# Linear attention in four chunks with a recurrent state, against one causal 256x256 score matrix per head

## The chip, the cores and the metric

The kernel runs on one core of a Trainium2 chip. The metric is device time in microseconds (us). The engines are PE (TensorE, matrix products), ACT (ScalarE), DVE (VectorE), POOL (GpSimd) and SP (SyncE, which issues the loads).

## The reference

Two transformer blocks over 256 tokens of width 2048, all in f32. The change touches one part of the second block, the gated linear attention: 4 heads, key width 256, value width 512, chunks of 64 tokens. Cut to what matters:

```python
def _gla_chunked(q, k, v, g):          # q is already scaled by 1/16
    b = jnp.cumsum(g, axis=2)          # within a chunk of 64
    b_mid = b[:, :, CHUNK // 2:CHUNK // 2 + 1]
    b_last = b[:, :, CHUNK - 1:CHUNK]
    a = jnp.einsum("bnihd,bnjhd->bnhij", q * jnp.exp(b - b_mid), k * jnp.exp(b_mid - b))
    a = jnp.where(jnp.tril(jnp.ones((CHUNK, CHUNK), dtype=bool)), a, 0.0)
    o_intra = jnp.einsum("bnhij,bnjhe->bnihe", a, v)
    q_in = q * jnp.exp(b)
    k_st = k * jnp.exp(b_last - b)
    decay = jnp.exp(b_last[:, :, 0])
    def step(state, xs):
        qn, kn, vn, dn = xs
        o = jnp.einsum("bihd,bhde->bihe", qn, state)
        state = state * dn[..., None] + jnp.einsum("bjhd,bjhe->bhde", kn, vn)
        return state, o
```

The output is o_intra plus the scanned o, then an RMS norm over the 512 values of a head, a gain and a gate.

## The kernel before

**Units.** Almost all of the run is matrix products of streamed weights. A *unit* is one 512 KB weight block of 512 x 256. SP loads it into one of five RAW slots (`load`, L326 to L345, which waits until the slot's earlier content was used); ACT rounds it to its high part WH (`act_split`, L433); DVE computes the low part WL (`dve_split`, L442); PE runs 8 pairs of matmuls (L394, L396) with it. WH and WL hold a ring of four units, so ACT and DVE split unit w + 4 in step w, and ACT's split waits until PE has finished unit w. Each engine has its own program in order. In one step w it does its part of the products, then the work placed beside unit w (`pe_beside`, `act_beside`, `dve_beside`). Four units make a pair of output tiles, which ACT (L509) and DVE (L534) move out of PSUM.

**The linear attention** rides beside the stages "og" and "g_a": 2 turns of 16 units each, one head per turn (heads 0, 1 in og, 2, 3 in g_a). `pe_linear_step`, `act_linear_step` and `dve_linear_step` get the unit w of the turn:

- w = 0 to 2: DVE and ACT make QMID, KMID (decays relative to the middle of a chunk), QIN, KEND (relative to its start and end) and DEND (a chunk's whole decay). L1441 ends that and raises gla_ready.
- w = 5: PE transposes KEND (L1310) and the values (L1314), and makes four 64x64 score blocks (L1320). ACT copies to KTOK, VTOK (L1382, L1383); DVE copies the causal half of the scores into AT (L1444).
- w = 8, 10, 12, 14: chunk c = 0 to 3. PE makes the state's new sum (L1337, not for c = 3) and per tile of 128 values the outputs, from AT (L1342) and from STATE (L1345, not for c = 0). DVE updates STATE (L1455, L1457).
- w = 14 and 15: ACT squares the output (L1386); PE sums the squares of four tiles with ONES (L1352); ACT takes Ln and Exp (L1390, L1392); DVE writes the normed output (L1464) and raises gla_normed.

In front of og stands `dve_decays` with the decay sums; behind og and g_a ACT applies Silu or Sigmoid to the stage's result (`act_gate`, L1476).

**The modulation** is a matrix-vector product on DVE, spread over the whole run: 12 blocks of 16 steps. A step (L1602, 1.3 us) takes one 512 KB load of its own through the same RAW slots. MOD_STEPS (L26 to L30) says at which units; a tuple gives units of each turn. `place_modulation` also places each block's end: PE sums over partitions (`pe_modulation`, L1613), one unit later DVE adds the bias (L1629). The sums go to a corner of OU[:, 1], which the linear attention uses too: so pe_modulation waits for gla_normed, and in head 2 PE's unit 5 waits for the block that ended in og (L1306).

```python
            total = unit + 2
            for name, following in (("og", "g_a"), ("g_a", "g_b")):
                if by_name[name].unit0 <= unit < by_name[following].unit0:
                    total = by_name[following].unit0 + 2
```

Of the kernel before, what the change touches and what calls it, by code (L numbers as in the profile page):

```python
# [11 lines left out]
P = 128  # L12
T = 256
# [14 lines left out]
    ("og", (3, 6, 9, 11, 14)), ("g_a", (3, 4, 6, 7, 9, 11, 13, 14)), ("g_b", 16), ("branch_a", 8),  # L28
# [188 lines left out]
def place_modulation(plan, stages, by_name):  # L217


    units = []  # L220
    for name, steps in MOD_STEPS:
        stage = by_name[name]
        if isinstance(steps, tuple):
            units += [stage.unit0 + i * stage.units + w for i in range(stage.turns) for w in steps]
            continue
        length = stage.pairs * stage.per_pair // (2 if name in ("mix_out", "down1") else 1)
        units += [stage.unit0 + (2 * j + 1) * length // (2 * steps) for j in range(steps)]
    assert len(units) == MOD_BLOCKS * KT
    plan.mod_steps, plan.mod_sums, plan.mod_adds = {}, {}, {}
    for n, unit in enumerate(units):  # L230
        plan.mod_steps.setdefault(unit, []).append(n)
        if n % KT == KT - 1:
            total = unit + 2
            for name, following in (("og", "g_a"), ("g_a", "g_b")):
                if by_name[name].unit0 <= unit < by_name[following].unit0:
                    total = by_name[following].unit0 + 2
            stage = next(stage for stage in stages if total < end_unit(stage))
            heads = stage.beside in ("diff", "mem", "win")
            if heads:
                total += (3 - (total - stage.unit0)) % stage.units  # L240
# [127 lines left out]
def pe_stage(pe, k, stage):  # L368
# [3 lines left out]
    def turn(i, last):  # L372
        for b in range(stage.body):
# [3 lines left out]
            for q in range(stage.per_pair):  # L377
# [21 lines left out]
                if stage.unit0 + i * stage.units + w in k.plan.mod_sums:  # L399
                    pe_modulation(pe, k, k.plan.mod_sums[stage.unit0 + i * stage.units + w], stage)  # L400
# [885 lines left out]
def blocks_before(k, name):  # L1286

    return sum(unit < k.plan.s[name].unit0 for unit in k.plan.mod_sums)
# [12 lines left out]
def pe_linear_step(pe, k, h, w):  # L1301

    if w == 5:

        pe.wait_ge(k.gla_ready, h + 1)
        if h == 2:  # L1306
            pe.wait_ge(k.mod_done, blocks_before(k, "g_a") + 1)
        for d in range(2):
            for tb in range(2):
                pe.transpose(k.SC[:, 0, tb * T + d * P:tb * T + d * P + P],  # L1310
                             k.KEND[:, d, tb * P:tb * P + P], k.IDENT[:, :])
        for e in range(GLA_DV_T):
# [12 lines left out]
    elif w in (8, 10, 12, 14):  # L1325
        c = (w - 8) // 2
        if c == 0:
            pe.wait_ge(k.gla_copied, h + 1)
            pe.wait_ge(k.gla_masked, h + 1)
        half, block = slice(64 * (c % 2), 64 * (c % 2) + 64), c // 2  # L1330
        if c:
            pe.wait_ge(k.state_ready, 3 * h + c)

            pe.wait_ge(k.chunk_out, 3 * h + c)
        if c < 3:
            for d in range(2):
                mm = pe.matmul(k.SC[:, d, :], k.KTOK[half, block, d * P:d * P + P],  # L1337
                               k.VTOK[half, block, :], start=True, stop=True)
            mm.then_inc(k.state_sum, 1)
        for e in range(GLA_DV_T):  # L1340
            out = k.OU[:, e // 2, (e % 2) * T + c * CHUNK:(e % 2) * T + c * CHUNK + CHUNK]
            mm = pe.matmul(out, k.VTOK[half, block, e * P:e * P + P],  # L1342
                           k.AT[half, block, :], start=True, stop=c == 0)
            for d in range(2) if c else ():
                mm = pe.matmul(out, k.STATE[:, d, e * P:e * P + P],  # L1345
                               k.QIN[:, d, c * CHUNK:c * CHUNK + CHUNK], start=False,
                               stop=d == 1)
        mm.then_inc(k.gla_out if c == 3 else k.chunk_out, 1)
    elif w == 15:
        pe.wait_ge(k.gla_squared, h + 1)  # L1350
        for e in range(GLA_DV_T):
            mm = pe.matmul(k.SC[:, 0, 0:T], k.ONES[:, :], k.OSQ[:, e, :], start=e == 0,  # L1352
                           stop=e == GLA_DV_T - 1)
        mm.then_inc(k.gla_summed, 1)
# [13 lines left out]
def act_linear_step(act, k, h, w, chain):  # L1368
# [11 lines left out]
    elif w == 5:  # L1380
        act.wait_ge(k.gla_turned, h + 1)
        act.activation(k.KTOK[:, :, :], k.SC[:, 0, :].rearrange("p (b d) -> p b d", b=2), ACT.Copy)  # L1382
        act.activation(k.VTOK[:, :, :], k.OU[:, :, :], ACT.Copy).then_inc(k.gla_copied, 1)  # L1383
    elif w == 14:
# [3 lines left out]
    elif w == 15:  # L1388
        act.wait_ge(k.gla_summed, h + 1)
        chain.link(act.activation(k.BREL[:, 0, :], k.SC[:, 0, 0:T], ACT.Ln,  # L1390
                                  scale=1.0 / (GLA_DV_T * P), bias=k.EPS[:, 0:1]))
        act.activation(k.BREL[:, 0, :], k.BREL[:, 0, :], ACT.Exp,  # L1392
                       scale=-0.5).then_inc(k.gla_rstd, 1)


def dve_decays(dve, k, chain):

    dve.memset(k.AT[:, :, :], 0.0)
# [24 lines left out]
def dve_linear_step(dve, k, h, w, chain):  # L1423
# [13 lines left out]
    elif w == 2:  # L1437
# [3 lines left out]
        dve.tensor_tensor(k.KEND[:, :, :], k.KEND[:, :, :], keys, ALU.mult).then_inc(k.gla_ready, 1)  # L1441
    elif w == 5:
        dve.wait_ge(k.gla_turned, h + 1)
        dve.copy_predicated(k.AT[:, :, :], k.TRIL[:, :, :].bitcast(I32),  # L1444
                            k.SC[:, 1, 0:P].rearrange("p (b i) -> p b i",
                                                      b=2)).then_inc(k.gla_masked, 1)
    elif w in (8, 10, 12):
        c = (w - 8) // 2
        dve.wait_ge(k.state_sum, 3 * h + (c + 1))
        if c:  # L1450
            dve.wait_ge(k.chunk_out, 3 * h + c + 1)
        for d in range(2):
            state = k.STATE[:, d, :]
            if c == 0:
                last = dve.tensor_scalar(state, k.SC[:, d, :], 1.0, None, ALU.mult)  # L1455
            else:
                last = dve.scalar_tensor_tensor(  # L1457
                    out=state, in0=state, scalar=k.DEND[:, 4 * d + c, :], in1=k.SC[:, d, :],
                    op0=ALU.mult, op1=ALU.add)
        last.then_inc(k.state_ready, 1)  # L1460
    elif w == 15:
# [144 lines left out]
def pe_modulation(pe, k, block, stage):  # L1606
# [3 lines left out]
    if stage.name in ("g_a", "g_b"):  # L1610
        pe.wait_ge(k.gla_normed, 2 if stage.name == "g_a" else GLA_HEADS)
# [55 lines left out]
def pool_second_constants(pool, k, chain):  # L1667
# [8 lines left out]
    pool.memset(k.TRIL[:, :, :], 1.0)  # L1676
# [7 lines left out]
    for half in range(2):  # L1684
        select(k.TRIL[64 * half:64 * half + 64, :, :], [[0, 2], [1, CHUNK]], 0, -1, 0.0,
               ALU.is_ge)
# [217 lines left out]
def make_semaphores(nc, k, ctx):  # L1904
# [29 lines left out]
    k.chunk_out = semaphore("chunk_out")  # L1934
# [34 lines left out]
    k.state_ready = semaphore("state_ready")  # L1969
    k.state_sum = semaphore("state_sum")  # L1970
    k.gla_out = semaphore("gla_out")
    k.gla_squared = semaphore("gla_squared")
    k.gla_summed = semaphore("gla_summed")
# [33 lines left out]
def place_buffers(nc, k, ctx):  # L2007

    base = (nc.sbuf_base + 63) // 64 * 64
    size = T * 4  # L2010

    class Region:
# [5 lines left out]
        def put(self, name, shape, dtype=F32, tile=0):  # L2018
# [36 lines left out]
    k.KTOK = y.put("KTOK", [P, 2, T], tile=6)  # L2055
    k.STATE = y.put("STATE", [P, 2, 2 * T], tile=8)
# [33 lines left out]
    k.GKL = dist.put("GKL", [P, T])  # L2090
    k.AT = nc.alloc_sbuf_tensor_at("AT", [P, 2, CHUNK], F32, offset=dist.start + size)
    k.TRIL = nc.alloc_sbuf_tensor_at("TRIL", [P, 2, CHUNK], F32,
                                     offset=dist.start + size + 2 * CHUNK * 4)
# [85 lines left out]
```

## Time and profile before

| | us |
|---|---|
| median of 3 runs | 2822.84 (2819.81 to 2824.84) |
| the profiled execution | 2834.41 |
| its span | 2832.7 |
| mean granted TensorE clock | 0.973 |
| busy in the span: PE, DVE, ACT, POOL | 2720.1 (96%), 1979.5 (70%), 1317.3 (47%), 11.5 (0%) |
| read from HBM | 551.18 MB, 195 GB/s over the span |

Busy time of PE counts overlapping matmuls once. The times of the profile belong to the one profiled execution, whose span is 0.4% above the median. "x4" behind a line is a count of instructions. PEclk is the TensorE clock that was granted, 1.00 for full speed.

### The profile page before, as it was taken

The page shows a single profiled execution, that of the slowest core. Times are in us where ns is not written, and L with a number is a line of the kernel's source. Part 1 is how long each engine was busy: PE and PEld are TensorE (multiplying, and loading weights), DVE is VectorE, ACT ScalarE, POOL GpSimd, SP SyncE. Part 2 cuts the span into 40 slices and gives each one's busy share as a digit, 9 for nine tenths or more (in the row PEclk, how much of TensorE's full clock was granted, in tenths as well). Part 3 has the DMA queues.
Part 4 walks back from the last instruction along what each step waited for, and adds up shares of the span by engine and source line. Part 5 has one row for each costly group of instructions (what it writes and reads, how often), then busy time and mean ns, then how long its engine had stood idle before and what let it go on. Part 6 is the DMA issues. An engine that isn't in the chain of part 4 may idle for free.

```text
span 2832.7 us, 38110 instructions
## 1 busy us (share of the span) xinstructions
PE 2720.1 (96%) x15225; PEld 2326.9 (82%) x15225; DVE 1979.5 (70%) x2606; ACT 1317.3 (47%) x1748; POOL 11.5 (0%) x63
## 2 busy tenths in 40 slices
PE   6999999999999998999999999999799999999997
PEld 6888888788888787888778888888688888888886
DVE  4777676777766777666555557878578887688864
ACT  5544555454555544454433444544444444444442
POOL 0000000000000100000000000000000000000000
PEclk9999999999999999999989999999899999999998
DMA  5687554678655476655345558888456669966662
GB/s 194 193 260 245 164 157 142 223 247 271 201 163 150 139 242 208 209 155 149 113 149 156 179 183 258 271 263 275 125 155 188 186 186 293 286 192 187 194 214 84
DMA packets 570762, 555.78 MB, mean 196 GB/s; under 512 B 18231, under 2 KB 545226, under 8 KB 569818
## 3 DMA queue, kind: packets, MB, share of 16 engines
q1 hardware_dynamic: 570586, 553.34, 63.3%
q8 instruction: 121, 1.98, 0.3%
q14 instruction: 55, 0.45, 0.0%
HBM read 551.18 MB, written 2.10 MB: 195 GB/s over the span
## 4 chain that ended last, share of the span: by engine, by line
PE 84%; DVE 9%; ACT 4%; issue 2%; SPq 0%; DMA 0%; POOL 0%; ACTq 0%; DVEq 0%; POOLq 0%
PE ACC L394 50%; PE ACC L396 25%; DVE WL L442 2%; ACT WH L433 1%; PE OU L1345 1%; PE OU L881 1%; ACT PROB L906 1%; PE SC L1337 1%; PE SC L649 1%; PE OU L1342 1%; PE SC L860 1%; PE SC L889 1%; PE OU L1613 1%; DVE PROB L936 1%; PE SC L848 1%
## 5 line engine op out<-in xcount | busy, mean ns | idle before, releaser
L394 PE MATMUL ACC<-XH,WH 128*128 128x512 f32 x6096 | 2198.9, 404 | 47.7 <-issue 22.1
L396 PE MATMUL ACC<-XH,WL 128*128 128x256 f32 x6096 | 1717.0, 282 | 0.0
L433 ACT ACTIVATE WH<-RAW 128x1024 fp32r<-128x1024 f32 x852 | 900.1, 1058 | 1318.1 <-PE ACC L396 1287.7
L442 DVE TENSOR_TENSOR WL<-RAW,WH 128x1024 fp32r<-128x1024 f32 x852 | 1035.7, 1221 | 682.8 <-ACT WH L433 680.0
L394 PEld LDWEIGHTS ACC<-XH,WH 128*128 128x128 f32 x6096 | 1159.7, 190 | 340.3 <-issue 44.0
L396 PEld LDWEIGHTS ACC<-XH,WL 128*128 128x128 f32 x6096 | 1165.0, 191 | 5.5 <-issue 3.8
L394 PE MATMUL ACC<-AH,WH 128*128 128x512 f32 x704 | 247.0, 396 | 0.0
L1602 DVE SCALAR_TENSOR_TENSOR MODACC<-RAWMOD,CACT,MODACC 128x1024 f32<-128x1024 f32 x180 | 230.3, 1279 | 0.0
L396 PE MATMUL ACC<-AH,WL 128*128 128x256 f32 x704 | 196.3, 279 | 0.0
L394 PEld LDWEIGHTS ACC<-AH,WH 128*128 128x128 f32 x704 | 132.1, 188 | 31.4
L396 PEld LDWEIGHTS ACC<-AH,WL 128*128 128x128 f32 x704 | 132.5, 188 | 0.1
L509 ACT ACTIVATE HIGH<-ACC 128x512 f32<-128x512 f32 (+1 forms) x211 | 113.1, 536 | 10.5 <-PE ACC L396 10.5
L529 DVE TENSOR_TENSOR PR<-ACC,HIGH 128x512 f32<-128x512 f32 x64 | 43.8, 684 | 2.3 <-ACT HIGH L509 2.3
L570 DVE SCALAR_TENSOR_TENSOR CV<-U,PARAM,CV 128x256 f32<-128x256 f32 x88 | 42.7, 485 | 3.1
L568 DVE SCALAR_TENSOR_TENSOR CV<-U,PARAM,CV 128x256 f32<-128x256 f32 x88 | 42.6, 485 | 3.1
L906 ACT ACTIVATE PROB<-PROB,NM 128x256 f32<-128x256 f32 x80 | 39.8, 499 | 5.9 <-DVE NM L945 4.6
L531 DVE TENSOR_TENSOR PR<-PR,RSTD 128x512 f32<-128x512 f32 x56 | 38.8, 692 | 1.9
L566 DVE TENSOR_SCALAR CV<-U,PARAM 128x256 f32<-128x256 f32 x88 | 36.4, 414 | 3.2
L565 DVE TENSOR_TENSOR U<-ACC,HIGH 128x256 f32<-128x256 f32 x88 | 36.8, 418 | 0.6 <-ACT HIGH L509 0.6
L649 PE MATMUL SC<-PR,ONES 128*128 128x256 f32 x64 | 20.8, 492 | 17.0 <-ACT PR L680 17.0
L543 DVE TENSOR_TENSOR SUM<-ACC,HIGH 128x512 f32<-128x512 f32 x40 | 27.4, 685 | 9.9 <-ACT HIGH L509 9.8
L1345 PE MATMUL OU<-QIN,STATE 128*128 128x64 f32 x192 | 33.6, 300 | 0.0
(254 smaller groups left out, 1362.8 us busy)
## 6 DMA issues: line engine op xcount, KB each, us to landing
RAW<-in_w_in SPq DMA_DIRECT2D x408, 512.0 KB, 4.5
RAWMOD<-in_w_mod SPq DMA_DIRECT2D x192, 512.0 KB, 4.8
RAW<-in_w_up SPq DMA_DIRECT2D x176, 512.0 KB, 4.6
RAW<-in_w_out SPq DMA_DIRECT2D x96, 512.0 KB, 4.8
RAW<-in_w_down SPq DMA_DIRECT2D x88, 512.0 KB, 4.8
RAW<-in_w_mem_kv SPq DMA_DIRECT2D x32, 512.0 KB, 4.3
RAW<-in_w_branch_gla SPq DMA_DIRECT2D x32, 512.0 KB, 5.0
RAW<-in_w_branch_attn SPq DMA_DIRECT2D x16, 512.0 KB, 5.0
```

The source lines that it names most:

```text
L394: pe.matmul(bank, k.WH[:, w % RING, kc, cols], x, start=tile == 0, stop=False)
L396: mm = pe.matmul(bank[:, 0:T], k.WL[:, w % RING, kc, cols], x[:, 0:T], start=False, stop=tile == tiles - 1)
L433: act.activation(k.WH[:, slot, :, 0:width], k.RAW[:, r % RAWS, :, 0:width], ACT.Copy).then_inc(k.hi_ready, 1)
L442: dve.tensor_tensor(k.WL[:, slot, :, 0:width], k.RAW[:, k.plan.unit_load[unit] % RAWS, :, 0:width], k.WH[:, slot, :, 0:width].bitcast(F32) ...
L509: act.activation(k.HIGH[:, first:stage.tiles], k.ACC[:, bank + first:bank + stage.tiles, T:2 * T], ACT.Copy).then_inc(k.high_ready, 1)
L529: chain.link(dve.tensor_tensor(dst, low, high, ALU.add))
L568: chain.link(dve.scalar_tensor_tensor(out=cv, in0=u[:, 1:1 + T], scalar=column(taps[1]), in1=cv, op0=ALU.mult, op1=ALU.add))
L570: dve.scalar_tensor_tensor(out=cv, in0=u[:, 0:T], scalar=column(taps[0]), in1=cv, op0=ALU.mult, op1=ALU.add).then_inc(done, 1)
L649: mm = pe.matmul(sums_of(k, n), k.ONES[:, :], squares_of(k, n, c)[:, f, :], start=c + f == 0, stop=c + f == 6)
L906: last = act.activation(k.PROB[:, g, :], source, ACT.Exp, bias=k.NM[:, g:g + 1], scale=scale, accum_out=k.SM[:, g:g + 1])
L1345: mm = pe.matmul(out, k.STATE[:, d, e * P:e * P + P], k.QIN[:, d, c * CHUNK:c * CHUNK + CHUNK], start=False, stop=d == 1)
L1602: dve.scalar_tensor_tensor(out=k.MODACC[:, :], in0=raw, scalar=c, in1=k.MODACC[:, :], op0=ALU.mult, op1=ALU.add).then_inc(k.mod_used, 1)
```

## The change

The state, its four sequential steps and the transposes of KEND go. In unit 5 PE now also computes the score blocks between different chunks: keys KEND of chunk c against QFAR, which holds the queries of all later chunks, decayed from the end of chunk c. DVE makes QFAR out of QIN and DEND ahead of gla_ready. All score blocks land in one bank of SC: 256 query columns for keys 0 to 127, and 128 query columns for keys 128 to 255. One masked copy takes them to AT, 384 columns wide, and in unit 8 PE applies them to all values: per value tile one matmul of 256 columns and one of 128. The square goes to unit 9 on ACT; DVE adds the four tiles of squares in unit 10; PE sums one tile in unit 11; Ln and Exp in unit 11, the normed output in unit 12. The last modulation steps of each turn move forward, and the blocks that end within og and g_a are summed in unit 14 of that turn.

```diff
-    ("og", (3, 6, 9, 11, 14)), ("g_a", (3, 4, 6, 7, 9, 11, 13, 14)), ("g_b", 16), ("branch_a", 8),
+    ("og", (3, 6, 7, 9, 12)), ("g_a", (3, 4, 6, 7, 8, 9, 11, 12)), ("g_b", 16), ("branch_a", 8),
...
             total = unit + 2
-            for name, following in (("og", "g_a"), ("g_a", "g_b")):
-                if by_name[name].unit0 <= unit < by_name[following].unit0:
-                    total = by_name[following].unit0 + 2
...
+            elif stage.beside == "gla":
+                total += (14 - (total - stage.unit0)) % stage.units
...
@@ pe_linear_step
         pe.wait_ge(k.gla_ready, h + 1)
-        if h == 2:
-            pe.wait_ge(k.mod_done, blocks_before(k, "g_a") + 1)
-        for d in range(2):
-            for tb in range(2):
-                pe.transpose(k.SC[:, 0, tb * T + d * P:tb * T + d * P + P],
-                             k.KEND[:, d, tb * P:tb * P + P], k.IDENT[:, :])
...
         for c in range(4):
-            half, block = slice(64 * (c % 2), 64 * (c % 2) + 64), c // 2
             for d in range(2):
-                mm = pe.matmul(k.SC[half, 1, block * CHUNK:block * CHUNK + CHUNK],
-                               k.KMID[:, d, c * CHUNK:c * CHUNK + CHUNK],
-                               k.QMID[:, d, c * CHUNK:c * CHUNK + CHUNK], start=d == 0,
+                pe.matmul(gla_scores(k, c, c, 1), k.KMID[:, d, c * CHUNK:c * CHUNK + CHUNK],
+                          k.QMID[:, d, c * CHUNK:c * CHUNK + CHUNK], start=d == 0, stop=d == 1)
+        for c, first in ((0, 0), (1, 3), (2, None)):
+            later = 3 - c
+            for d in range(2):
+                q = (k.QIN[:, d, 3 * CHUNK:] if first is None else
+                     k.QFAR[:, d, first * CHUNK:(first + later) * CHUNK])
+                mm = pe.matmul(gla_scores(k, c, c + 1, later),
+                               k.KEND[:, d, c * CHUNK:c * CHUNK + CHUNK], q, start=d == 0,
                                stop=d == 1)
         mm.then_inc(k.gla_turned, 1)
-    elif w in (8, 10, 12, 14):
...
+    elif w == 8:
+        pe.wait_ge(k.gla_copied, h + 1)
+        pe.wait_ge(k.gla_masked, h + 1)
         for e in range(GLA_DV_T):
+            out = k.OU[:, e // 2, (e % 2) * T:(e % 2) * T + T]
+            pe.matmul(out, k.VTOK[:, 0, e * P:e * P + P], k.AT[:, 0:T], start=True, stop=False)
+            mm = pe.matmul(out[:, P:T], k.VTOK[:, 1, e * P:e * P + P], k.AT[:, T:T + P],
+                           start=False, stop=True)
+        mm.then_inc(k.gla_out, 1)
+    elif w == 11:
+        pe.wait_ge(k.gla_presummed, h + 1)
+        pe.matmul(k.SC[:, 0, 0:T], k.ONES[:, :], k.OSQ[:, 0, :], start=True,
+                  stop=True).then_inc(k.gla_summed, 1)
+
+def gla_scores(k, keys, queries, count):
+    first = queries * CHUNK if keys < 2 else T + (queries - 2) * CHUNK
+    return k.SC[CHUNK * (keys % 2):CHUNK * (keys % 2) + CHUNK, 1, first:first + count * CHUNK]
...
@@ act_linear_step
     elif w == 5:
-        act.activation(k.KTOK[:, :, :], k.SC[:, 0, :].rearrange("p (b d) -> p b d", b=2), ACT.Copy)
...
-    elif w == 14:
+    elif w == 9:
         act.wait_ge(k.gla_out, h + 1)
...
-    elif w == 15:
+    elif w == 11:
         act.wait_ge(k.gla_summed, h + 1)
...
@@ dve_linear_step, w == 2
         dve.wait_ge(k.end_exps, h + 1)
-        dve.tensor_tensor(k.KEND[:, :, :], k.KEND[:, :, :], keys, ALU.mult).then_inc(k.gla_ready, 1)
+        chain.link(dve.tensor_tensor(k.KEND[:, :, :], k.KEND[:, :, :], keys, ALU.mult))
+        far = k.QFAR[:, :, :].rearrange("p d (c t) -> p d c t", c=5)
+        q = k.QIN[:, :, :].rearrange("p d (c t) -> p d c t", c=4)
+        ends = k.DEND[:, :, :].rearrange("p (d c) n -> p d c n", d=2)
+        dve.tensor_copy(far[:, :, 0:4:3, :], q[:, :, 1:3, :])
+        chain.link(dve.tensor_tensor(far[:, :, 1:5:3, :], q[:, :, 2:4, :],
+                                     ends[:, :, 1:3, :].broadcast_to([P, 2, 2, CHUNK]), ALU.mult))
+        dve.tensor_tensor(far[:, :, 2, :], far[:, :, 4, :],
+                          ends[:, :, 1, :].broadcast_to([P, 2, CHUNK]),
+                          ALU.mult).then_inc(k.gla_ready, 1)
     elif w == 5:
...
+        dve.copy_predicated(k.AT[:, :], k.TRIL[:, :].bitcast(I32),
+                            k.SC[:, 1, 0:T + P]).then_inc(k.gla_masked, 1)
+    elif w == 10:
+        dve.wait_ge(k.gla_squared, h + 1)
+        chain.link(dve.tensor_tensor(k.OSQ[:, 0:2, :], k.OSQ[:, 0:2, :], k.OSQ[:, 2:4, :], ALU.add))
+        dve.tensor_tensor(k.OSQ[:, 0, :], k.OSQ[:, 0, :], k.OSQ[:, 1, :],
+                          ALU.add).then_inc(k.gla_presummed, 1)
+    elif w == 12:
         dve.wait_ge(k.gla_rstd, h + 1)
...
@@ pe_modulation
-    if stage.name in ("g_a", "g_b"):
-        pe.wait_ge(k.gla_normed, 2 if stage.name == "g_a" else GLA_HEADS)
+    if stage.beside == "gla":
+        pe.wait_ge(k.gla_normed, head)
```

The rest of the diff follows from this: `pe_stage` passes the head to pe_modulation; the DVE steps that updated STATE (w = 8, 10, 12) and their semaphores are gone; TRIL, the mask, is [128, 384] now and POOL selects it in two pieces (columns 0 to 255 and the rest); in the SBUF, QFAR and AT take the place of KTOK and STATE, TRIL that of DIST, and GKL gets a region of its own.

## Rows read from the trace of the kernel before

**Rows 1.** The page's part 4, the chain that ended last, share by engine.
```profile
PE 84%; DVE 9%; ACT 4%; issue 2%; SPq 0%; DMA 0%; POOL 0%; ACTq 0%; DVEq 0%; POOLq 0%
```
**Rows 2.** Windows, four heads, then g_b: us, busy PE PEld DVE ACT POOL, PEclk, DMA, GB/s.
```profile
1424.25:1502.30 78.05, 77.65 (x403) 64.39 (x403) 43.40 (x51) 27.46 (x34) 0.00 (x0) 0.89 0.52 157
1502.30:1576.65 74.35, 73.44 (x401) 60.88 (x399) 35.58 (x42) 30.66 (x36) 0.00 (x0) 0.93 0.48 144
1576.65:1644.90 68.25, 68.25 (x386) 56.76 (x387) 40.38 (x47) 26.87 (x32) 0.00 (x0) 0.97 0.58 186
1644.90:1705.00 60.10, 60.10 (x340) 49.46 (x339) 35.20 (x38) 23.41 (x26) 0.00 (x0) 0.97 0.58 187
1705.00:1790.00 85.00, 85.00 (x487) 73.96 (x487) 62.66 (x59) 39.99 (x43) 0.00 (x0) 1.00 0.87 277
```
**Rows 3.** Windows of head 1: through chunk 0, and right behind chunk 1.
```profile
1511.95:1517.95 6.00, 6.00 (x31) 4.36 (x30) 3.62 (x5) 1.06 (x1) 0.00 (x0) 1.00 0.88 274
1526.95:1529.95 3.00, 3.00 (x11) 2.62 (x11) 1.41 (x2) 0.00 (x0) 0.00 (x0) 0.50 0.25 85
```
**Rows 4.** Chain in order of time, head 1: start us, us, engine, output, line, count.
```profile
1502.30 0.44 PE SC L1310 x4
1502.74 0.87 PE OU L1314 x8
1503.61 0.66 PE SC L1320 x16
...
1512.95 1.91 PE SC L1337 x4
1514.86 0.84 PE OU L1342 x8
...
1523.46 0.17 PE OU L1342 x2
1523.63 0.59 PE OU L1345 x4
1524.22 0.36 PE OU L1342 x2
...
1555.27 1.74 PE SC L1352 x8
```
**Rows 5.** Unit 13 of head 0 (ACT, DVE); group of L1345 weight loads, mean ns second.
```profile
1475.50 1.06 ACT L433 ACTIVATE WH<-RAW 128x1024 fp32r<-128x1024 f32 x1 [1.71 <-PE ACC L396]
1477.73 1.28 DVE L1602 SCALAR_TENSOR_TENSOR MODACC<-RAWMOD,CACT,MODACC 128x1024 f32<-128x1024 f32 x1
...
L1345 PEld LDWEIGHTS OU<-QIN,STATE 128*128 128x128 f32 x192 | 26.7, 201 | 3.3
```
**Rows 6.** PE in order of time, heads 0 and 2; in brackets idle us before it, releaser.
```profile
1427.62 0.66 PE L1310 MATMUL SC<-IDENT,KEND 128*128 128x128 f32 x4 [0.40 <-DVE KEND L1441]
...
1565.31 1.84 PE L1613 MATMUL OU<-ONES,MODACC 128*128 128x1 f32 x16
1576.65 0.63 PE L1310 MATMUL SC<-IDENT,KEND 128*128 128x128 f32 x4 [0.91 <-DVE MODS L1629]
```
**Rows 7.** DVE groups by form: count, busy us, mean ns of one, idle us before.
```profile
L664 DVE TENSOR_TENSOR PR<-PR 128x512 f32<-128x512 f32 x12 | 8.2, 685 | 0.0
L666 DVE TENSOR_TENSOR PR<-PR 128x256 f32<-128x256 f32 x12 | 5.1, 425 | 0.4
L1223 DVE COPY VS<-PR 128x256 f32<-128x256 f32 x12 | 3.5, 290 | 0.0
```
**Rows 8.** ACT and DVE in order of time: gates behind og, KEND of head 2.
```profile
1560.41 3.91 ACT L1476 ACTIVATE PR<-PR 128x1024 f32<-128x1024 f32 x4 [0.66 <-DVE PR L534]
...
1574.61 0.69 DVE L1441 TENSOR_TENSOR KEND<-KEND,PR 128x512 f32<-128x512 f32 x1
```
**Rows 9.** ACT groups: table loads in front of Ln; busy us, mean ns, idle us.
```profile
L1390 ACT ACT_TABLE_LOAD x2 | 2.6, 1283 | 0.0
```
**Rows 10.** DVE in order of time, in front of head 0.
```profile
1401.10 1.66 DVE L1401 TENSOR_SCALAR DECAY<-SC,PARAM 128x256 f32<-128x256 f32 x4 [7.21 <-PE OU L1296]
```

More of the change, by code:

```diff
@@ L399, in turn @@
                 if stage.unit0 + i * stage.units + w in k.plan.mod_sums:
-                    pe_modulation(pe, k, k.plan.mod_sums[stage.unit0 + i * stage.units + w], stage)
+                    pe_modulation(pe, k, k.plan.mod_sums[stage.unit0 + i * stage.units + w], stage,
+                                  stage.first + i + 1)
                 pe_beside(pe, k, stage, i, w)
@@ L1323, in pe_linear_step @@
+        for c, first in ((0, 0), (1, 3), (2, None)):
[5 more added lines that the diff above has]
+                               k.KEND[:, d, c * CHUNK:c * CHUNK + CHUNK], q, start=d == 0,
                                stop=d == 1)
         mm.then_inc(k.gla_turned, 1)
-    elif w in (8, 10, 12, 14):
[L1326 to L1339, printed above, removed]
-        for e in range(GLA_DV_T):
[L1341 to L1348, printed above, removed]
-    elif w == 15:
[L1350 to L1354, printed above, removed]
@@ L1387, in act_linear_step @@
                        ACT.Square).then_inc(k.gla_squared, 1)
-    elif w == 15:
+    elif w == 11:
         act.wait_ge(k.gla_summed, h + 1)
@@ L1396, in dve_decays @@
 def dve_decays(dve, k, chain):
-    dve.memset(k.AT[:, :, :], 0.0)
+    dve.memset(k.AT[:, :], 0.0)
     dve.wait_ge(k.decay_logits, 1)
@@ L1440, in dve_linear_step @@
         dve.wait_ge(k.end_exps, h + 1)
-        dve.tensor_tensor(k.KEND[:, :, :], k.KEND[:, :, :], keys, ALU.mult).then_inc(k.gla_ready, 1)
+        chain.link(dve.tensor_tensor(k.KEND[:, :, :], k.KEND[:, :, :], keys, ALU.mult))
[8 more added lines that the diff above has]
+                          ALU.mult).then_inc(k.gla_ready, 1)
     elif w == 5:
         dve.wait_ge(k.gla_turned, h + 1)
[L1444 to L1461, printed above, removed]
+        dve.copy_predicated(k.AT[:, :], k.TRIL[:, :].bitcast(I32),
[6 more added lines that the diff above has]
+    elif w == 12:
         dve.wait_ge(k.gla_rstd, h + 1)
@@ L1603, in dve_modulation, with pe_modulation @@
                                  op0=ALU.mult, op1=ALU.add).then_inc(k.mod_used, 1)
-def pe_modulation(pe, k, block, stage):
+def pe_modulation(pe, k, block, stage, head):
     pe.wait_ge(k.mod_used, KT * (block + 1))
     wait_from_zero(pe, k.mod_done, block)
-    if stage.name in ("g_a", "g_b"):
-        pe.wait_ge(k.gla_normed, 2 if stage.name == "g_a" else GLA_HEADS)
+    if stage.beside == "gla":
+        pe.wait_ge(k.gla_normed, head)
     for c in range(MOD_COLS // P):
@@ L1675, in pool_second_constants @@
     pool.memset(k.RESET[:, :], 1.0)
-    pool.memset(k.TRIL[:, :, :], 1.0)
+    pool.memset(k.TRIL[:, :], 1.0)
     for m in (k.DUP, k.DUPROT):
@@ L1683, in pool_second_constants @@
            ALU.not_equal)
-    for half in range(2):
-        select(k.TRIL[64 * half:64 * half + 64, :, :], [[0, 2], [1, CHUNK]], 0, -1, 0.0,
-               ALU.is_ge)
+    for first, count in ((0, T), (T, P)):
+        select(k.TRIL[:, first:first + count], [[1, count]], 0, -1, 0.0, ALU.is_ge)
     for parity in range(2):
@@ L1933, in make_semaphores @@
     k.gate_conv = semaphore("gate_conv")
-    k.chunk_out = semaphore("chunk_out")
     k.presummed = semaphore("presummed")
@@ L1968, in make_semaphores @@
     k.gla_masked = semaphore("gla_masked")
-    k.state_ready = semaphore("state_ready")
-    k.state_sum = semaphore("state_sum")
     k.gla_out = semaphore("gla_out")
     k.gla_squared = semaphore("gla_squared")
+    k.gla_presummed = semaphore("gla_presummed")
     k.gla_summed = semaphore("gla_summed")
@@ L2054, in place_buffers @@
     k.KEND = y.put("KEND", [P, 2, T], tile=4)
-    k.KTOK = y.put("KTOK", [P, 2, T], tile=6)
-    k.STATE = y.put("STATE", [P, 2, 2 * T], tile=8)
+    k.QFAR = y.put("QFAR", [P, 2, 5 * CHUNK], tile=6)
+    k.AT = y.put("AT", [P, T + P], tile=9)
     k.DECAYS = [None, y.put("DECAY1", [P, GLA_T // 2, T], tile=12)]
@@ L2089, in place_buffers @@
     k.DIST = dist.put("DIST", [P, 2, T])
[L2090 to L2093, printed above, removed]
+    k.TRIL = dist.put("TRIL", [P, T + P])
+    k.GKL = Region(size).put("GKL", [P, T])
     k.DISTI = pr.put("DISTI", [P, 2, T], I32, tile=44)
```

## The prediction, made before the changed kernel ran

> **What bounds the kernel now.** I read the page's chain first: what ended last is 84% TensorE (PE), so time that PE stops spending is time off the run unless something else comes late [rows 1]. The change touches only the two stages "og" and "g_a", which carry the four linear-attention heads, one head per sixteen units. Next the windows, one per head, from one head's transposes (unit 5) to the next's (the first from 1424.25, the last to just after g_a): 78.1, 74.4, 68.3 and 60.1 us, PE busy 98% or more of each, and a granted clock of only 0.89, 0.93, 0.97, 0.97 [rows 2]. A clock of 1.00 is the 2.4 GHz level and 0.50 the 1.2 GHz one. The reader should see two costs: work, and a clock lost. Time lost is length times (1 - clock): 8.6 + 5.2 + 2.0 + 1.8 = 17.6 us (each clock is rounded to 0.005, so within 0.4 us a head). A short window says where: right behind a chunk step of head 1 the clock is 0.50 with PE busy 3.00 of 3 us, while it is 1.00 through chunk 0 and what follows that [rows 3]. Then the chain of waits through head 1 gives the PE time of each piece of a head without the overlap that the busy figures hold [rows 4]. All f32 matmuls appear as two instructions; a transpose as one.
>
> **What is removed, per head, at full clock** [rows 4]. In unit 5: KEND transposes, 0.44. Chunk 0: state sums 1.91, outputs 0.84. Chunk 1 and chunk 2 each: state sums 1.91, then per value tile a pair on AT at 0.36 (the first, 0.17) and four on STATE at 0.59: 1.91 + 0.17 + 3 x 0.36 + 4 x 0.59 = 5.52. Chunk 3 has no state sum: 4 x 0.36 + 4 x 0.59 = 3.80. The square sums over four tiles: 1.74. Sum: 0.44 + 2.75 + 5.52 + 5.52 + 3.80 + 1.74 = 19.77 us. The eight V transposes (0.87) and the 16 near-score instructions (0.66) stay. That leaves, of head 2's 68.25 us, 68.25 - 19.77 - 1.53 - 2.0 (clock) = 44.95 for sixteen units of products, 2.81 each. As a check, head 1's window must then hold 44.95 + 21.30 + 5.2 (clock) + 0.91 (a wait) + 1.84 (a modulation sum) = 74.2; it is 74.35 [rows 2, 6].
>
> **What is added, per head.** Far scores in unit 5: six f32 matmuls, twelve instructions, with 192, 128 and 64 query columns, four of each. Unseen in this form. Square sums of 256 columns take 1.74/8 = 0.217 us each; near scores of 64 columns into halves of the partitions 0.66/16 = 0.041 [rows 4]. From below, 4 x (3 + 2 + 1) x 0.041 = 1.0; from above, all twelve at 0.217 = 2.6. I take width times 0.217/256: 4 x (0.163 + 0.109 + 0.054) = 1.3, since the many-column ones carry most. Outputs in unit 8: per value tile two instructions of 256 columns and two of 128. The first at 0.217. For 128 columns the neighbours are 0.109 by width (a transpose's 0.87/8 = 0.109 agrees) and 0.147, which 64-column matmuls with full weights take (0.59/4) [rows 4]; I take 0.147, as the weights must be loaded anyway: 4 x (0.434 + 0.294) = 2.9, between 2.6 and, all at 0.217, 3.5. Square sum in unit 11: two instructions, 0.43. Sum 4.63, between 4.0 and 6.5. **Work saved: 19.77 - 4.63 = 15.1 us a head, 60.5 us in four** (53 to 63).
>
> A rule to weigh: the 80 small instructions of the chunk outputs (8, then 3 x 24) cost 0.84 + 2 x 3.61 + 3.80 = 11.9 us a head by the chain, 0.148 each, while a weight load itself is shown with 201 ns [rows 4, 5]. The Trainium skill, "TensorE: Matmul & The Clock Gate", section "LDWEIGHTS (loading the stationary operand)", gives columns / 1.2 ns, 107 ns for 128 columns; priced so, an estimate, the 80 would be 8.6 us and the saving 3.3 us a head smaller, some 13 us in all (about 47 instead of 60.5). The trace disagrees with that price for f32 weights, and the measured rows stand.
>
> **Clock.** The 0.50 stretch of head 1 lies behind a chunk step of 24 small instructions after 1.9 us of state sums; chunk 0 (2.75 us) leaves the clock at 1.00 [rows 3, 4]. The change keeps one small-tile stretch of 0.87 + 0.66 + 1.3 = 2.8 us in unit 5 and puts 2.9 us of wide, full-array matmuls in unit 8. Both are about as long as chunk 0's, and half of the chunk steps' 5.5. I take 14 of the 17.6 us as returned; what stays is two losses of the size that heads 2 and 3 have now (1.8 us each) [rows 2]. Bounds: all 17.6, or nothing (as many drops behind the new steps).
>
> **DVE before unit 5.** Three operations join ahead of gla_ready, each behind a link or KEND: a 256-element copy (0.29), a 256-element product (0.42), a 128-element one (0.3, by width between nothing and the 256's) [rows 7], and two links: 1.1 us (0.7 to 1.5). Heads 1 and 3 hide it: DVE does this at unit 2 and PE asks after unit 5, and of the four heads only two show a wait there. Head 0 waits 0.40 us for KEND already, so +1.1. Head 2 is late as well, 0.91 us [rows 6]. There the chain runs: ACT and DVE finish head 1 (L1464), evacuate (L534), four Silu activations, then 11.0 us from their end (1564.32) to KEND's end (1575.3) [rows 8]. After the change L1464 is done in unit 12; after unit 15's products (1555.27 in the chain, the start of the square sums) come ACT's split, its copy and DVE's addition, and the Silus start some 3 us on instead of 5.1 [rows 4, 8]. Done: 3.0 + 3.9 + 11.0 + 1.1 = 19.0 after unit 15, while PE has six units, 16.9 us: wait 2.1 instead of 0.9, +1.2. The modulation sums (1.84) that PE did at head 2's unit 2 move to head 1's unit 14, at equal cost, and so does the block behind g_a.
>
> **The presum.** ACT squares in unit 9, DVE adds in unit 10, PE asks after unit 11. From the end of a unit's products, ACT's split ends at 1.15, DVE's at 2.3 (head 0's unit 13: ACT starts 1475.50, DVE's next work 1477.73) [rows 5]; two additions of 0.69 and 0.43 [rows 7] and a link make 3.5, while PE's unit is 2.81: 0.7 us of wait a head, 2.8 in all (0 to 6; DVE's modulation steps of units 8 and 9 could push it). Behind this wait on PE are units 12 on; their splits are four units ahead, so nothing else comes late.
>
> **Unit 14.** In head 3 Ln and Exp need two table loads of 1.28 [rows 9]; DVE's four gain products wait for them and the last modulation step of unit 12 is behind those. By the same stepping it ends 0.8 us after PE asks for it in unit 14: +0.8. In head 1 there are no loads, no wait.
>
> **At nothing:** removed state updates on DVE and the KTOK copy on ACT (under PE's units); the masked copy of 384 instead of 128 elements (three units to spare); DVE's larger memset (DVE waits 7.21 us behind it) [rows 10]; POOL's two wider selections (they lie with the other constants in the layer before). DMA: each moved modulation step takes its load along in SP's queue; in g_a ten unit loads and eight of these fall into units 3 to 12. The four-unit ring hides it: heads run at 144 to 187 GB/s and the next stage moves 277 with PE at 100% [rows 2]. Over g_a, 48 loads of 0.524 MB in two heads of 52 us are 242 GB/s. If that cover failed, DVE would wait in front of a modulation step, and its presum and evacuation behind it: rival (c).
>
> **Sum:** -60.5 - 14 + 1.1 + 1.2 + 2.8 + 0.8 = **-68.6 us**. The profiled execution took 2834.4 (span 2832.7), 0.4% over the median of 2822.84; on its own clock 2765.8, on the median 2754.2.
>
> **Rivals.** (a) *The clock does not come back*: the remaining steps drop it as often. Against: head 1's chunk 0 doesn't; for: unit 5's stretch gets 0.8 us longer and keeps its transposes. Then -54.6: 2768. Here belongs a rule: The Trainium skill, same page, section "Why this matters for your kernels", advises against idle gaps between bursts of matmuls to avoid throughput drops; by it alone these stretches, which have none, should lose no clock, and removing them should give none back. By that rule the result is this rival's 2768; the trace disagrees, since PE is busy 3.00 of 3.00 us at 0.50 [rows 3]. Chance 0.20. (b) *All clock back, no new wait* but head 0's: -77: 2746. For: DVE may run its link faster; against: stepping is plain. Chance 0.17. (c) *Loads or DVE become the bound in g_a*: modulation steps in units 6 to 9 hold DVE and its presum. DVE is busy 40 of 68 us in head 2 [rows 2] and would be about 39 of 52. At 4 us more per g_a head and 1 per og head, -59: 2764. Chance 0.10. (d) *Slower*: gla_ready comes so late that PE stands before unit 5 in each head. The break-even is 68.6/4 = 17 us a head against 1.1 us added to DVE's chain, so it needs an operation some ten times its row. 2830; chance 0.01. (e) *It doesn't do what it says*: PE's freed time is eaten by a hidden bound at half the gain: 2788; against, PE's 98% in every window. Chance 0.02. Forecast 0.50.
>
> **Range.** 2741 to 2776: from all clock back with the low added work, no new wait and the two old ones gone (-63 - 17.6 - 1.3 = -82) to no clock back and the added work at its upper bound (-53 + 5.9 = -47). It holds (a), (b) and (c); about 0.15 stays outside, (d), (e) and the tails. A measurement of this kernel tells about 0.2%, 5.6 us, from no change. Faster takes all cases but (d), 0.01, and 0.01 kept for a gain lost whole: 0.98, 0.01, 0.01.
>
> **What would show it.** Windows of og and g_a heads of about 52 us; the unit-8 group near 0.22 and 0.15 us an instruction; granted clock 0.98 or more; PE waits of 0.7 on DVE's addition in unit 11 and of about 1.5 and 2 before unit 5 in heads 0 and 2. A clock still near 0.93 makes (a) right; a PE wait on WL or a DMA wait in front of DVE's modulation (c). The forecast is wrong if the heads stay above 56 us, or if the stages behind g_a give time back.

## The result, and the profile of the changed kernel

The changed kernel takes 2759.99 us (median of 4 runs, 2757.4 to 2763.8) against 2821.57 for the one before: a ratio of 0.9765, 95% interval 0.9744 to 0.9787. That is 61.6 us less by the medians, 66 by the ratio; 68.6 was forecast (2754.2), with a range of 2741 to 2776. Sent again beside other runs, it gave 2757.81 against 2825.79, ratio 0.976 (0.974 to 0.9779).

The profiled execution took 2757.4 us, span 2755.5: 77 us under the profiled execution of before. The windows of the four heads, cut as in [rows 2] (us, busy PE PEld DVE ACT POOL, PEclk, DMA share, GB/s):

```profile
1421.20:1475.99 54.79, 52.84 (x325) 45.81 (x324) 39.94 (x50) 25.68 (x32) 0.00 (x0) 1.00 0.72 220
1475.99:1532.00 56.01, 53.12 (x327) 45.80 (x325) 34.24 (x43) 30.06 (x35) 0.00 (x0) 1.00 0.62 191
1532.00:1585.42 53.42, 52.72 (x312) 45.76 (x313) 40.11 (x46) 26.46 (x31) 0.00 (x0) 0.97 0.76 243
1585.42:1632.00 46.58, 45.29 (x287) 39.50 (x285) 34.65 (x38) 26.02 (x28) 0.00 (x0) 1.00 0.75 237
```

The heads are 51 to 56 us apart where they were 68 to 75, and the clock is 1.00 but for a dip in head 2. The windows average 52.7 us, where about 52 was forecast; head 1's, which holds a modulation sum and head 2's wait, is at the 56 that was named as the limit. PE now idles a little, though (head 1's window: 2.9 us). What it waited for, and the new work, in PE's order of time (heads 0, 2 and 3):

```profile
1424.59 1.09 PE L1308 MATMUL OU<-IDENT,PR 128*128 128x128 f32 x8 [1.19 <-DVE QFAR L1435]
1425.62 0.73 PE L1313 MATMUL SC<-QMID,KMID 128*64 128x64 f32 x16
1426.13 0.82 PE L1320 MATMUL SC<-QFAR,KEND 128*64 128x192 f32 x8
...
1447.55 0.70 PE L1335 MATMUL SC<-OSQ,ONES 128*128 128x256 f32 x2 [0.76 <-DVE OSQ L1445]
...
1531.99 1.09 PE L1308 MATMUL OU<-IDENT,PR 128*128 128x128 f32 x8 [2.08 <-DVE QFAR L1435]
...
1617.72 1.95 PE L1599 MATMUL OU<-ONES,MODACC 128*128 128x1 f32 x16 [0.54 <-DVE MODACC L1588]
```

The waits stand where the prediction put them: before unit 5 in heads 0 and 2 (1.19 and 2.08 us), in unit 11 (0.70 to 0.76 in each head), in unit 14 of head 3 (0.54). The chain gives the pieces without overlap, to be held against [rows 4] (start, us, engine, output, line, count):

```profile
1475.99 0.87 PE OU L1308 x8
1476.86 0.66 PE SC L1313 x16
1477.52 0.83 PE SC L1320 x11
...
1487.03 0.43 PE OU L1329 x2
1487.46 0.22 PE OU L1330 x2
```

The far scores take 0.83 us, the outputs, four times 0.43 + 0.22, 2.62 from the first to the next product, the square sum 0.43 (by the chain of the kernel narrow, below, where PE doesn't wait in front of it).

### The profile page after: what moved, and what is told of

Same layout as the page of the kernel before. It is cut to its first block, busy times and chain, and to the rows that moved or that the text cites. A ratio compares the mean times of both kernels' runs of the same rounds, so it can differ in the third digit from the quotient of the medians.

```text
span 2755.5 us, 37486 instructions
## 1 busy us (share of the span) xinstructions
PE 2635.5 (96%) x14929; PEld 2266.8 (82%) x14929; DVE 1972.4 (72%) x2602; ACT 1314.8 (48%) x1744; POOL 11.6 (0%) x63
## 4 chain that ended last, share of the span: by engine, by line
PE 82%; DVE 10%; ACT 5%; issue 2%; SPq 0%; DMA 0%; POOL 0%; ACTq 0%; DVEq 0%; POOLq 0%
PE ACC L393 50%; PE ACC L395 25%; DVE WL L442 2%; ACT WH L433 2%; PE OU L881 1%; ACT PROB L906 1%; PE SC L649 1%; DVE PROB L936 1%; PE OU L1599 1%; PE SC L860 1%; DVE MX L939 1%; PE SC L889 1%; DVE MODACC L1588 0%; PE SC L848 0%; DVE Y L1479 0%
## 5 line engine op out<-in xcount | busy, mean ns | idle before, releaser
L509 ACT ACTIVATE HIGH<-ACC 128x512 f32<-128x512 f32 (+1 forms) x211 | 113.1, 536 | 10.2 <-PE ACC L395 10.2
L529 DVE TENSOR_TENSOR PR<-ACC,HIGH 128x512 f32<-128x512 f32 x64 | 43.7, 683 | 2.3 <-ACT HIGH L509 2.3
L534 DVE TENSOR_TENSOR PR<-ACC,HIGH 128x512 f32<-128x512 f32 x46 | 31.4, 684 | 4.2 <-ACT HIGH L509 4.2
```

The source lines that it names most:

```text
L509: act.activation(k.HIGH[:, first:stage.tiles], k.ACC[:, bank + first:bank + stage.tiles, T:2 * T], ACT.Copy).then_inc(k.high_ready, 1)
L529: chain.link(dve.tensor_tensor(dst, low, high, ALU.add))
```

## The experiments

All ratios are to the kernel before, timed beside it on the same chip; the medians of different rows can come from different chips. "Clock lost in the heads" is length times (1 - granted clock), summed over windows of 2 us from the first head's scores to the end of the last head. It belongs to the one profiled execution.

| kernel | median us | ratio to before, 95% interval | clock lost in the heads, us |
|---|---|---|---|
| before, sent again | 2821.13 | 1.0006 (0.9989 to 1.0023) | 10.2 (first profile 17.1) |
| changed, sent again | 2757.81 | 0.9760 (0.9740 to 0.9779) | 3.4 (first profile 1.7) |
| split_steps | 2828.34 | 1.0025 (1.0004 to 1.0047) | 10.2 |
| wide | 2816.51 | 0.9988 (0.9968 to 1.0008) | 1.7 |
| narrow | 2821.17 | 0.9997 (0.9978 to 1.0016) | 12.0 |
| narrow13 | 2809.98 | 0.9927 (0.9902 to 0.9952) | 1.7 |
| chunk_shape | 2840.60 | 1.0056 (1.0034 to 1.0079) | 18.8 |
| old_mod | 2754.97 | 0.9734 (0.9710 to 0.9757) | 0.0 |
| presum9 | 2757.89 | 0.9758 (0.9739 to 0.9778) | 6.8 |
| scores6 | 2758.44 | 0.9763 (0.9739 to 0.9787) | 1.7 |
| both | 2753.45 | 0.9738 (0.9718 to 0.9759) | 1.7 |
| sum15 | 2747.27 | 0.9712 (0.9686 to 0.9738) | 0.0 |

**Both kernels again.** No edit.

> The kernel before once more, with its own profile. Theory 1 (its clock loss in the heads varies between executions, and the first profile, 0.4% above the median, caught a bad one): a loss well under 17.6 us, 5 to 13, with a span near 2820. Rival (the loss is fixed, and the profiled execution was long for another reason): 17 to 18 us again.

> The changed kernel once more, as the yardstick for the three runs beside it. Theory 1 (the profiles of before and after differ by their clock losses in the heads, which vary from one execution to the next): about 2760 us, 60 to 66 us under before, and in the profile a clock loss in the four heads of 0 to 4 us, not always behind the same unit. Theory 2 (a fixed loss tied to head 2's wait): 1.7 us lost in head 2 again and nothing elsewhere.

Before lost 10.2 us in the heads this time and 17.1 in the first profile, and its span was 2820.3. So the first profile had caught an execution with much clock lost: 7 us more in the heads, and 7 more in front of them, where both kernels are the same. The changed kernel lost 3.4 us, at other places than in its first profile: behind head 0's unit 5, where PE had waited 2.09 us, and behind head 3's modulation sum. Head 2's wait, 2.09 us as well, passed without a dip. So the dips are not tied to head 2, but they do go with the length of the wait: over all profiles of this study, PE waited 2.04 to 2.09 us in front of unit 5 nine times, and eight times the clock fell to the 1.2 GHz level there; of thirteen waits of 0.40 to 1.70 us in the same place none was followed by a fall. The 14 us more of lost clock in the first profile of before are why the two first profiles differ by 77 us and the medians by 62 to 68.

**split_steps.** The kernel before, cut differently. PE's state sums stay in units 8, 10 and 12; the outputs of the four chunks come in units 8, 11, 13 and 14, and DVE updates STATE in units 8, 11 and 13:

```diff
-    elif w in (8, 10, 12, 14):
+    elif w in (8, 10, 11, 12, 13, 14):
...
+        if w in (8, 11, 13, 14):
...
-    elif w in (8, 10, 12):
+    elif w in (8, 11, 13):
```

> The kernel before, with the outputs of chunks 1 and 2 moved one unit behind their state sums (units 11 and 13), so that no stretch of small matmuls is longer than 3.8 us; nothing is left out. Theory 1 (a long stretch of small matmuls lowers the clock): most of the loss in the heads goes, 6 to 14 us less than before, at the same PE work. Rival (what counts is the narrow work as such, however it is cut): as before within 3 us.

The rival was right about the clock: the loss is what the uncut kernel lost in its second profile, 10.2 us. The time is 0.25% longer, some 7 us and more than the rival's 3; the two more interruptions a head explain about 2 of them by the rows, the rest is open. A window over the outputs alone of head 0's chunk 1, 3.8 us of work from 1447.1, and what follows (same columns as above):

```profile
1448.00:1457.00 9.00, 9.00 (x37) 7.43 (x37) 4.43 (x5) 0.94 (x3) 0.00 (x0) 0.62 0.38 110
```

PE is busy throughout, and yet the clock averages 0.62: outputs without the state sums directly in front of them are enough to lower it. The first profile of before already showed this, and the prediction passed over it: chunk 3 has no state sums, and behind its 3.8 us of outputs in head 0 (from 1475.33) stands

```profile
1480.00:1482.00 2.00, 2.00 (x8) 1.71 (x8) 0.00 (x0) 0.47 (x1) 0.00 (x0) 0.50 1.01 314
```

In the profiles of before, before_again and split_steps together, the clock fell at or behind 8 of 20 such stretches of outputs alone.

**wide and narrow.** Work is added to the changed kernel in units 10, 12 and 14, its results unused:

```diff
@@ wide
+    elif w in (10, 12, 14):
+        for n in range(13):
+            pe.matmul(k.SC[:, 1, 0:T], k.VTOK[:, 0, (n % 4) * P:(n % 4) * P + P], k.AT[:, 0:T],
+                      start=True, stop=True)
@@ narrow
+    elif w in (10, 12, 14):
+        for d in range(2):
+            pe.matmul(k.SC[:, 1, :], k.VTOK[0:64, 0, d * P:d * P + P], k.VTOK[0:64, 0, :],
+                      start=True, stop=True)
+        for e in range(GLA_DV_T):
+            for n in range(3):
+                pe.matmul(k.SC[:, 1, n * CHUNK:n * CHUNK + CHUNK],
+                          k.VTOK[:, 0, e * P:e * P + P], k.AT[:, n * CHUNK:n * CHUNK + CHUNK],
+                          start=True, stop=True)
```

> As the narrow one, but each of the twelve additional pieces is thirteen f32 matmuls of 256 columns with full weights, about 5.6 us; its results are not used. Theory 1: 12 x 5.6 = 68 us more than the changed kernel and a clock of 1.00 behind them. Rival (any interruption of the products by 5 us lowers the clock): the same loss as the narrow one, 5 to 17 us on top.

> The changed kernel with additional work in units 10, 12 and 14 of each head, shaped like a chunk step of before: two f32 matmuls of 512 columns with 64 rows, then twelve of 64 columns with full weights; its results are not used. At full clock 12 x 5.5 = 66 us more than the changed kernel. Theory 1 (narrow matmuls lower the clock): 5 to 17 us on top of that, and a clock of 0.50 behind these steps in the profile. Rival (the clock comes back for another reason, such as the state's updates on DVE being gone): nothing on top.

The wide pieces lower nothing behind them: 5.6 us of interruption by full-width matmuls leaves the clock alone, and the loss of 1.7 us is again one dip at head 2's unit 5, where PE waits for QFAR. Their cost, 64 us by the ratios (59 by the medians, which come from different chips), is the 68 of work less the 3 us of unit-11 waits that the longer unit 10 covers. With the narrow pieces 12.0 us were lost, 1.7 of them again at head 2's unit 5, but not as theory 1 had it. A piece was cheaper than a chunk step, 24 instructions in 2.82 us instead of 3.61, and ten of the twelve left the clock at 1.00. It fell only at the two in unit 14 that came right behind a modulation sum (a wide piece in the same place left it at 1.00, both times). Chain and window of such a plain piece, then the window over a piece beside a sum:

```profile
1523.32 1.91 PE SC L1335 x4
1525.23 2.82 PE SC L1339 x24
```
```profile
1525.23:1531.00 5.77, 5.77 (x41) 5.36 (x42) 3.35 (x6) 0.00 (x0) 0.00 (x0) 1.00 0.57 155
1535.30:1546.00 10.70, 10.70 (x39) 8.46 (x39) 0.86 (x1) 0.00 (x0) 0.00 (x0) 0.56 0.28 89
```

**narrow13 and chunk_shape.** The first moves the third narrow piece to unit 13. The second keeps units 10, 12, 14 and gives the twelve narrow matmuls the rows of a real chunk step; its two matmuls of 512 columns use rows 64 to 127 instead of 0 to 63:

```diff
@@ narrow13
-    elif w in (10, 12, 14):
+    elif w in (10, 12, 13):
@@ chunk_shape, in place of the loop over n
+            out = k.SC[:, 1, 0:CHUNK]
+            pe.matmul(out, k.VTOK[half, 0, e * P:e * P + P], k.AT[half, CHUNK:2 * CHUNK],
+                      start=True, stop=False)
+            for d in range(2):
+                pe.matmul(out, k.VTOK[:, d, e * P:e * P + P],
+                          k.QIN[:, d, CHUNK:2 * CHUNK], start=False, stop=d == 1)
```

> The narrow one with its third piece in unit 13 instead of 14, so that none stands next to a modulation sum. Theory 1 (in the narrow one the clock fell only where a piece followed the sum's sixteen one-column matmuls): no loss behind the pieces, under 3.5 us in the heads against 12.0. Rival (it falls behind any piece now and then): two or three drops again at other places.

> As the narrow one, but with the row counts of a real chunk step: of the twelve 64-column matmuls behind the two of 512 columns, four use 64 rows and eight use 128, alternating as before. Theory A (mixing 64-row and 128-row matmuls is what slows the pieces and lowers the clock): 24 instructions take 3.6 us instead of the narrow one's 2.9, and the clock is at 0.50 behind three or more steps besides those next to a modulation sum; 8 us of work more than the narrow one and a loss of 8 to 17 us in the heads. Theory B (the 64 columns do it, whatever the rows): as the narrow one, drops only beside the modulation sums.

Both came out as theory 1 and theory A said. With no piece beside a modulation sum the loss is 1.7 us, all of it at head 2's unit 5. With the rows mixed it is 18.8 us, but not all of that is due to the mixing: 1.7 us are head 2's unit 5, and 10.2 stand at the two pieces beside a modulation sum, about what the narrow kernel lost there too. What the mixed rows add is the 6.8 us behind four of the ten pieces that stand alone; of the narrow kernels' 22 pieces that stand alone none was followed by a fall.

This does not hang on one profile: the whole run's granted clock was 0.980 or 0.981 in all four runs of narrow13, 0.975 to 0.978 in all ten of narrow and 0.971 to 0.975 in all eight of chunk_shape. By the ratios chunk_shape takes 17 us more than narrow, which has its pieces in the same units: 9.5 us of work (12 x 0.79) and 6.8 of clock.

The chain of chunk_shape in head 1, and the window right behind it:

```profile
1515.31 1.91 PE SC L1336 x4
1517.22 0.17 PE SC L1340 x2
1517.39 0.59 PE SC L1343 x4
1517.97 0.36 PE SC L1340 x2
1518.34 0.59 PE SC L1343 x4
```
```profile
1521.00:1524.50 3.50, 3.50 (x13) 3.02 (x12) 0.00 (x0) 0.00 (x0) 0.00 (x0) 0.52 0.11 39
```

It repeats the old pattern of [rows 4] number for number. A pair with 64 rows takes 0.36 us between pairs with 128 rows, and 0.17 directly behind another with 64; the narrow instructions that all use 128 rows take 2.82/24 = 0.117 each. In all, the 24 mixed instructions take 3.61 us and the 24 plain ones 2.82: some 0.2 us for each of the four times that PE goes into 64 rows and back, 0.8 us per chunk step. The Trainium skill, "TensorEngine Tiling (Array Packing)", section "Tiling Modes", says that changing the tiling mode drains TensorE; this trace agrees with that, by those 0.2 us, though it does not show a drain as such. More differs between the two kernels: the moving operand of eight matmuls (QIN instead of AT), their accumulation, and the rows of the 512-column matmuls. None was tried alone, so that it is the row count is likely and not shown. The greater length of a mixed piece (5.5 us against 4.7) is not needed to lower the clock, since the mixed outputs alone do it in 3.8 us.

**old_mod.** The changed kernel with MOD_STEPS, the place of the sums and their waits as before:

```diff
-    ("og", (3, 6, 7, 9, 12)), ("g_a", (3, 4, 6, 7, 8, 9, 11, 12)), ("g_b", 16), ("branch_a", 8),
+    ("og", (3, 6, 9, 11, 14)), ("g_a", (3, 4, 6, 7, 9, 11, 13, 14)), ("g_b", 16), ("branch_a", 8),
...
```

> The changed kernel with the modulation put back: steps at the old units, sums at unit 2 of the next stage, head 2 waiting for the block's end. Theory 1 (moving it cost nothing and gained nothing, as forecast): 2758 within 4 us; 1.84 us of PE work returns to head 2's start, where PE waited 2.1 us anyway. Rival (the move is a part of the gain): 3 to 8 us slower than the changed kernel, through waits on DVE behind late steps.

No slower; its interval overlaps the changed kernel's. In its profile head 2's wait is 1.7 us for the modulation instead of 2.1 for QFAR, and the sum's 1.84 us sit in front of that wait. So the move is no part of the gain. Its lower median may come in part from elsewhere: in the feed-forward stages, where the kernels are equal and PE waits for nothing, the two matmuls of a pair showed 393 and 277 ns in this profile and 399 and 281 in that of the changed kernel.

```profile
L394 PE MATMUL ACC<-XH,WH 128*128 128x512 f32 x607 | 210.5, 393 | 0.0
```
```profile
L393 PE MATMUL ACC<-XH,WH 128*128 128x512 f32 x596 | 210.6, 399 | 0.0
```

Over 176 units of 2.8 us such a difference makes some 7 us. It is no property of this kernel: in this stage the profiles of both and wide show the lower figure too and the other eleven the higher, and within one profile it changes; before ran at 399 ns from 2100 to 2300 us and at 394 from 2500 to 2600. What sets it no run here tells.

**presum9, scores6, both, sum15.** Taking the new waits away one by one:

```diff
@@ presum9: dve_linear_step
-    elif w == 10:
+    elif w == 9:
         dve.wait_ge(k.gla_squared, h + 1)
@@ scores6: pe_, act_ and dve_linear_step
-    if w == 5:
+    if w == 6:
@@ sum15 (with the two above): place_modulation
-                total += (14 - (total - stage.unit0)) % stage.units
+                total += (15 - (total - stage.unit0)) % stage.units
```

> DVE adds the squares in unit 9 instead of unit 10. Theory 1 (PE's wait in unit 11 is DVE's place in unit 10 alone: ACT's squares end about 2.1 us after unit 9's products and DVE is free at 2.3): the four waits of 0.70 to 0.76 us go, about 2.9 us less than the changed kernel, 2757. Rival: ACT's squares come later than DVE, so DVE stands in unit 9 and its modulation step behind it; then the waits move to unit 12 or 14 and the time stays at 2760.

> PE's transposes and score blocks, ACT's copy and DVE's masked copy go from unit 5 to unit 6. Theory 1 (QFAR, made by DVE ahead of gla_ready, is what PE waits for in heads 0 and 2): the waits of 1.19 and 2.08 us go, and with the second the clock lost right behind it (1.7 us): 3.3 to 5 us less, about 2756. Rival: the values are needed in unit 8, two units later, and ACT or DVE is late there: a new wait of 1 us or so a head in unit 8, the time unchanged or 2 us longer.

> The two edits together. If they are independent, as theory 1 has it, 6 to 8 us less than the changed kernel, about 2753, and PE idle in the four heads only for the modulation sum of head 3. If one wait hides the other: 3 us less.

> Both edits, and the two blocks of modulation that end in og and g_a summed by PE in unit 15 instead of unit 14. Theory 1 (the 1.56 us that PE waited there for DVE's last modulation step is the only wait left in the heads): that wait goes, about 1.5 us less than both edits alone, 2752, no PE wait in the heads in the profile. Rival: DVE's bias addition, now in the first unit of the next stage, delays its splits there, behind the gates: the time stays.

By profile every one took its own wait away, but a part came back elsewhere. presum9 has no wait in unit 11, but head 3's wait for the modulation sum is 1.56 us instead of 0.54. scores6 has none in front of the scores, but in unit 11 head 2 waits 1.58 us instead of 0.70. With both, PE waits in the heads only for the modulation sum (1.56 us) and, once, 0.38 us for a split; with sum15 not at all, and it is busy for the whole stretch at full clock:

```profile
1425.00:1632.00 207.00, 207.00 (x1289) 182.24 (x1288) 154.70 (x179) 110.58 (x128) 0.00 (x0) 1.00 0.76 238
```

By time, the single edits can't be told from the changed kernel (2757.89 and 2758.44 against 2757.81). Both together give 4.4 us less, but the intervals overlap (0.9718 to 0.9759 against 0.9740 to 0.9779). sum15 is the fastest kernel of the study: 2747.27 us, ratio 0.9712, with an interval that ends just below where the changed kernel's begins (0.9738 against 0.9740). It was timed on another chip than that one; beside old_mod, which ran on the same chip, its interval overlaps (old_mod 0.9710 to 0.9757). So that the waits are gone is shown, and that their removal is worth their 5 to 7 us of time is likely. The rival of sum15, late splits in the next stage, did not show.

## Why the prediction was right

**The work.** 15.1 us a head were forecast, and 19.77 - 0.83 - 2.62 - 0.43 = 15.9 came. The far scores had been taken by width at the rate of full-array matmuls (1.3 us); they came below their lower bound of 1.0, at 0.83. Their weights are 64 columns wide, as the near scores' are (128*64 in both rows above), and the near scores too run faster than by width (0.041 us against 0.054); that this is the reason was not tried. The 128-column outputs ran at 0.11 us an instruction, the neighbour by width (0.109), and not at 0.147. The other neighbour was misread: its 0.147 was not the price of loading 128 columns of weights, as I wrote, since 64-column matmuls with full weights take 0.117 when no 64-row ones stand between them. For the same reason the price of 107 ns for such a load in the Trainium skill, "TensorE: Matmul & The Clock Gate", section "LDWEIGHTS (loading the stationary operand)", which I set aside, is nearer to the truth than I allowed: the narrow pieces' 117 ns comes close to it, and what made the old steps dearer was most likely the switches between row counts.

**The clock.** In the two first profiles 17.1 us fell to 1.7, a little over the 14 forecast. But the 17.6 us I started from was one bad execution. A second one lost 10.2 us, and the second profile of the changed kernel 3.4. By these the return is more like 7 to 9 us; what is usual, two profiles of each kernel can't say. Rival (a), nothing returned, was wrong, and so was the rule beside it, of the Trainium skill, "TensorE: Matmul & The Clock Gate", section "Why this matters for your kernels", taken alone: split_steps and chunk_shape lose clock with PE busy throughout. That idle time costs clock too is seen in front of unit 5, where it fell at eight of nine waits of 2 us. What I named as its cause, long stretches of small matmuls, was half right. Cutting them in two did not help; what lowers it are small matmuls that alternate 64 and 128 rows, or a narrow piece beside sixteen one-column matmuls. The two losses of 1.8 us that I left in the sum as what heads 2 and 3 had before came (1.7 each, one or two a profile), but mostly for another reason, the new wait of 2 us before unit 5, which I had forecast as a wait and not as a cause of lost clock.

**The waits.** Forecast: 1.1 more in head 0, 1.2 more in head 2, 2.8 in unit 11, 0.8 in unit 14, 5.9 together. Measured against the same places in [rows 6]: 0.8, 1.2, 2.9 and 0.54, together 5.4.

**The sum.** On the profiles: 4 x 15.9 + 15.4 - 5.4 = 73.6, and the distance from the last product before the first head's unit 5 to the gates of g_b shrank by 73.4; the other 3.8 of the 77 us lie in front of the heads, where the clock lost was 3.3 us less. On the medians 8 us of clock take the place of 15: 63.6 + 8 - 5.4 = 66, which is what the ratio gives (the two pairs of medians, 61.6 and 68.0, lie around it). That the forecast of 68.6 came so close is in part luck: two errors partly cancelled, 3 us too little work saved and 6 us too much clock. Rival (b) allowed no new wait but head 0's, and PE waits in every head. Rivals (c) to (e) did not occur: DMA moved 220 to 243 GB/s in three of the heads without holding PE.

## What to carry to other kernels

A recurrence over short chunks can be worth undoing where the sequence is no longer than the key width, as here (256 and 256): four dependent steps of narrow matmuls cost 19.8 us a head, and one wide masked score matrix does the same in 3.9. By the shapes it is also less work, some 31 million multiplications a head for the far scores and outputs against 59 million for the state sums and outputs; so narrowness is not all of the gain, and for a longer sequence the count would turn. Price narrow matmuls from rows with the same neighbours, and look whether matmuls of different row counts alternate. When a profile is 0.4% above the median of the runs, take a second one before its clock losses enter a sum. And when a stretch gets shorter, step each handoff between engines once more: waits appeared or grew in three places, and moving three handoffs by one unit each removed them all, though the first two, each alone, made another wait longer. Look too at what a wait does to the clock behind it.

## What the runs showed of the hardware that I had not expected

- Alternating f32 matmuls of 64 and of 128 rows cost some 0.2 us for each excursion to 64 rows (0.36 us a pair against 0.17), and the granted clock fell to the 1.2 GHz level behind four of the ten such pieces that stood alone, while PE was never idle. The same number of 64-column matmuls with 128 rows throughout left it at the 2.4 GHz level in all 22 pieces that stood alone.
- Right behind sixteen one-column matmuls, narrow pieces of either kind lowered it each time (four of four, 10.2 us in each of the two kernels).
- Thirteen f32 matmuls of 256 columns in the place of such a piece, 5.6 us, never lowered it, not beside the one-column matmuls either.
- Eight of nine waits of 2.04 to 2.09 us in front of unit 5 were followed by a fall of the clock, and none of thirteen waits of 0.40 to 1.70 us there.
- Identical product stages ran 1.5% apart in two executions (393 against 399 ns a matmul) at the same granted clock of 1.00. With the clock lost here and there this may make the scatter of 10 us and more among the runs of one kernel; it was not traced to either.
